# Attention in a hybrid S5 and sliding-window block: four buffers for transposed P, and the transposes ahead of P times V

## What is computed

```python
ATTN_PATTERNS = ((128, 1), (512, 4), (2048, 16))       # window, dilation; 8 heads of 64 each
proj = rmsnorm(x, norm_mix_g) @ w_in                    # u for the S5 branch, q k v, two gates
q = rmsnorm(q, q_norm_g) * scale;  k = rmsnorm(k, k_norm_g)
# per pattern and head, in blocks of 128 queries against the 256 keys that end with them
s = q_blk @ k_blk.T + bias                              # causal window and slope per head
p = exp(s - max(s));  den = sum(p);  o = (p @ v_blk) / den;  lse = max(s) + log(den)
o_attn = sum over patterns of softmax(lse) * o
```

## Time and profile before

| | |
|---|---|
| time, median of 3 runs | 1765.79 us (1765.23 to 1767.33) |
| the profiled execution | 1766.91 us |
| its span, first to last instruction | 1764.8 us |
| PE busy | 1720.0 us, 97% |
| DVE, ACT, POOL busy | 61%, 38%, 51% |
| PE waiting for ACT ptr L1601 | 5.4 us ahead of L1204, 1.6 us ahead of L1215 |
| attention stage | about 50 to 650 us of the span |

### The profile page before, as it was taken

The page is one execution under the profiler, slowest core; times in us unless marked ns, Lnnn a source line. Parts: engine busy times, 40 slices in busy tenths (PEclk is TensorE's granted clock), DMA queues, the critical chain, the costliest instruction groups (busy, mean ns, idle before and its releaser), DMA issues.

```text
span 1764.8 us, 23387 instructions
## 1 busy us (share of the span) xinstructions
PE 1720.0 (97%) x8316; PEld 1376.5 (78%) x8316; DVE 1073.0 (61%) x1553; ACT 664.5 (38%) x1263; POOL 902.9 (51%) x668
## 2 busy tenths in 40 slices
PE   8999999999999987999999999999999999999999
PEld 6777777777777765788887788788888888888887
DVE  6444555564455558443316632688778778748999
ACT  6653455445345521111411121443333333344443
POOL 7545463635544356664276754255545545445554
PEclk9999999999999998999999999999999999999999
DMA  4111321321132034444576534323223222385443
GB/s 180 37 43 34 96 79 43 90 67 55 30 99 73 25 97 109 121 121 121 217 250 245 194 131 166 132 99 104 71 71 93 85 71 73 137 274 165 138 144 126
DMA packets 89690, 198.84 MB, mean 113 GB/s; under 512 B 16560, under 2 KB 34096, under 8 KB 89600
## 3 DMA queue, kind: packets, MB, share of 16 engines
q1 hardware_dynamic: 78496, 190.19, 33.5%
q10 hardware_dynamic: 10640, 5.84, 1.4%
q0 software_dynamic: 464, 1.62, 0.2%
HBM read 152.31 MB, written 44.12 MB: 111 GB/s over the span
## 4 chain that ended last, share of the span: by engine, by line
PE 73%; DVE 14%; DMA 4%; POOL 3%; issue 2%; ACT 2%; SPq 0%; DVEq 0%; POOLq 0%; ACTq 0%
PE bank L1069 13%; PE bank L1071 12%; PE bank L1070 12%; PE bank L1422 7%; PE bank L1424 7%; PE bank L1423 7%; DVE dalo L2321 3%; DMA ab<-wgt_scr 2%; PE bank L1204 2%; PE bank L1215 2%; PE bank L1487 1%; PE bank L1488 1%; PE bank L1486 1%; PE bank L1188 1%; DMA raw<-in_wblocks 1%
## 5 line engine op out<-in xcount | busy, mean ns | idle before, releaser
L1069 PE MATMUL bank<-hhi,whi 128*128 128x512 f32 x1024 | 419.2, 409 | 11.6 <-DVE zb L1975 4.5
L1071 PE MATMUL bank<-hhi,wlo 128*128 128x512 f32 x1024 | 405.9, 396 | 0.0
L1070 PE MATMUL bank<-hlo,whi 128*128 128x512 f32 x1024 | 405.6, 396 | 0.0
L784 POOL TENSOR_TENSOR wlo<-raw,whi 128x1024 fp32r<-128x1024 f32 (+1 forms) x84 | 198.1, 2358 | 380.1 <-DVE whi L1859 378.6
L1069 PEld LDWEIGHTS bank<-hhi,whi 128*128 128x128 f32 x1024 | 194.0, 189 | 59.5 <-issue 6.6
L1071 PEld LDWEIGHTS bank<-hhi,wlo 128*128 128x128 f32 x1024 | 193.7, 189 | 45.9
L1070 PEld LDWEIGHTS bank<-hlo,whi 128*128 128x128 f32 x1024 | 194.5, 190 | 40.0 <-issue 0.2
L1058 POOL TENSOR_TENSOR dwlo<-dw_raw,dwhi 128x512 fp32r<-128x512 f32 x77 | 112.0, 1457 | 104.0 <-ACT dwhi L1751 104.0
L1614 ACT ACTIVATE sp<-sp,sd 128x128 f32<-128x128 f32 (+1 forms) x192 | 84.3, 440 | 117.4 <-DVE sd L2039 117.1
L1486 PE MATMUL bank<-dahi,dwhi 128*128 128x512 f32 x308 | 119.9, 389 | 0.0
L1487 PE MATMUL bank<-dalo,dwhi 128*128 128x512 f32 x308 | 119.8, 389 | 0.0
(11 more groups left out here) (319 smaller groups left out, 3739.3 us busy)
## 6 DMA issues: line engine op xcount, KB each, us to landing
raw<-in_wblocks SPq DMA_DIRECT2D x76, 512.0 KB, 4.4
pair<-in_wblocks SPq DMA_DIRECT2D x40, 512.0 KB, 4.8
ws<-in_wblocks SPq DMA_DIRECT2D x22, 512.0 KB, 5.3
wsum_scr<-ws SPq DMA_DIRECT2D x22, 512.0 KB, 3.9
ff_scr<-ffo SPq DMA_DIRECT2D x22, 512.0 KB, 5.9
dw_raw<-wsum_scr SPq DMA_DIRECT2D x44, 256.0 KB, 2.7
ff<-ff_scr SPq DMA_DIRECT2D x36, 256.0 KB, 4.1
dw_raw<-in_wblocks SPq DMA_DIRECT2D x33, 256.0 KB, 3.2
```

The source lines that it names most:

```text
L784: pool.tensor_tensor(wlo[par][:, 0:cols], raw[par][:, 0:cols], whi[par][:, 0:cols].bitcast(F32), ALU.subtract).then_inc(lo_done, 1)
L1069: nc.tensor.matmul(ps, a, x, start=start and k == k_list[0], stop=False)
L1070: nc.tensor.matmul(ps, a, y, start=False, stop=False)
L1071: last = nc.tensor.matmul(ps, b, x, start=False, stop=stop and k == k_list[-1])
```

## The change

`ptr` gets four buffers in place of two: a second tensor of the same size, `ptr_b`, is allocated beside scratch of the attention stage. ScalarE's copy and P times V choose the buffer by the block number modulo 4. On PE the transposes of block j-2 are moved ahead of P times V of blocks j-4 and j-3 within the sub-step. All waits stay with their instructions.

```diff
@@ tensors
-            ptr = sb("ptr", [P, 2, HT])
+            ptr_a = sb("ptr_a", [P, 2, HT])
...
+                ptr_b = sb("ptr_b", [P, 2, HT])
...
+        ptr = [x[:, i, :] for x in (ptr_a, ptr_b) for i in range(2)]
@@ PE, slot
+                        if 2 <= j < 10:
+                            s_ = j - 2
+                            pe.wait_ge(exp_done, 8 * a + s_ + 1)
+                            if a or s_:
+                                pe.wait_ge(tev, 8 * a + s_)
+                            for x in range(2):
+                                for kb in range(keys(ag, s_) // P, 2):
+                                    c = (2 * x + kb) * P
+                                    last = nc.tensor.transpose(b_t[:, c:c + P], sp[:, s_ % 4, x, kb * P:(kb + 1) * P], ident)
+                            last.then_inc(t_done, 1)
                         if j in (4, 6, 8, 10):
...
-                                                                ptr[:, s_ % 2, c:c + P], start=kb == k0, stop=kb == 1)
+                                                                ptr[s_ % 4][:, c:c + P], start=kb == k0, stop=kb == 1)
                                 last.then_inc(pv_done, 1)
-                        if 2 <= j < 10:
...
-                            last.then_inc(t_done, 1)
@@ ACT, slot
-                        src, dst = (... for x in (b_t[:], ptr[:, s_ % 2, :]))
+                        src, dst = (... for x in (b_t[:], ptr[s_ % 4]))
```

More of the change, by code:

```diff
@@ L1599, in slot @@
                         act.wait_ge(t_done, 8 * a + s_ + 1)
-                        src, dst = (x.rearrange("p (h q) -> p h q", h=2)[:, :, keys(ag, s_):] for x in (b_t[:], ptr[:, s_ % 2, :]))
+                        src, dst = (x.rearrange("p (h q) -> p h q", h=2)[:, :, keys(ag, s_):] for x in (b_t[:], ptr[s_ % 4]))
                         act.activation(dst, src, ACT.Copy).then_inc(tev, 1)
```

## The result

The changed kernel takes 1775.12 us in the median (1774.24 to 1777.44), the kernel before, measured beside it, 1766.56: a ratio of 1.0050 with a 95% interval of 1.0035 to 1.0065. Measured a second time it took 1775.58 us against 1767.38, a ratio of 1.0055 (1.0034 to 1.0076). The ratios here are not exactly those of the medians: the medians alone differ by 8.6 and 8.2 us, the ratios by 0.50% and 0.55% (8.8 and 9.7 us), each with an interval of 2.6 to 3.7 us to either side. The prediction was 1774.6.

What follows compares the result with a forecast made beforehand. PE, busy for 97% of the span, was taken to bound the kernel. The terms 1.9 + 3.5 + 3.5 = 8.9 us, on the scale of the median 1765.79, gave 1774.6 us, range 1768.0 to 1779.5.

Steps and rivals of the forecast that it cites:

- What bounds the kernel: Whole span: PE is busy for 97%, so a microsecond on its queue is normally one of the total.
- the no-change rival: Waits behind the attention stage, for zb and wlo, take up the loss: 1765.8 to 1768 us; chance 0.13.
- (a) The switch: Unstalled j = 4 and 6: entering the split array behind full-array transposes costs 0.17 us, eleven times, 1.9 us.
- The cover for the other five sub-steps: At j = 4 of slots 2, 3, 5, 6, 8 the loss falls into a later wait and costs nothing.
- (b) Stalls that lost their cover: Copy waits inside P times V, slots 2, 3, 5, 6, 8, 9: 0.49 to 0.74 us each, together 3.5.
- (c) The hidden wait: At j = 8 of eight slots, transposes wait for a copy the first PV half covered: 3.5 us.
- The last slot: PE gains 2.3 us at j = 4, 6 and 8, given no value because later waits grow.
- the sum: Slots 0 to 10: switches 1.9, stalls 3.5 and j = 8 waits 3.5 make 8.9 us, 0.5%.
- the two signs that would have shown the theory wrong: Exponentials starting earlier relative to S at j = 4 or 6, or transposes to PV under 0.4 us.
- Early copies: Attention stage: earlier transposes bring later copies forward and the eight stalls go, giving 1762.5 us; chance 0.08.
- The clock: Behind the two long waits, more PE idling prolongs the low clock, at most 3.5 us: 1778; chance 0.12.

Runs made afterwards that it cites:

- the split order: Against the kernel with only the four buffers: transposes put between the two halves of P times V; 1773.81 us against 1766.46, ratio 1.0050.
- the second trace: The changed kernel run and traced once more, with nothing altered; measured a second time at 1775.58 us against 1767.38, ratio 1.0055.
- the first experiment: Kernel before with four buffers for the transposed P, transposes still behind P times V; 1765.92 us against 1765.99, ratio 1.0001.
- early copies: ScalarE's copy ahead of its squares: kernel before 1769.41, again 1767.52 us; changed kernel 1770.26; kernel before, j = 3 and 5 only, 1764.03.

## Why the prediction was right, point by point

**What bounds the kernel.** PE's time was added to the total one for one. From the start of the last slot to the end of the wait for wlo it took 65.3 us before and 64.8 after, 65.3 with the new order in the last slot alone. In all thirteen traces it is 64.7 to 65.3 us, while the wait for zb varies from 2.5 to 5.2. That end follows the slot's start and not PE's arrival, so the no-change rival falls: the 10.3 us of slots 0 to 10 all arrive behind.

**(a) The switch.** Forecast 0.17 us in eleven sub-steps, 1.9 us. Ten of the eleven show 0.15 to 0.20 and sum to 1.6; the eleventh, j = 6 of slot 9, holds a stall. The Trainium skill ("TensorEngine Tiling (Array Packing)", Tiling Modes, Key Properties) has a change of tiling mode drain the engine; the 0.58 us in place of 0.41 agrees with it, and so do the two extra switches of the split order. The cover for the other five sub-steps held in four: slots 3 and 6 took the loss at j = 4 back at j = 6, slot 8 at j = 5, and slot 5 had none (-0.30 and 0.17 at j = 4 and 5). The fifth, slot 2, is below.

**(b) Stalls that lost their cover.** Forecast 0.49 each for slots 2, 5 and 8: measured 0.47, 0.46, 0.45. Forecast 0.74 for slots 3 and 6: measured 0.81 and 0.63, by both stalled sub-steps together, of which 0.5 stands at j = 4 and the rest at j = 6. Slot 9 at j = 4: forecast 0.53, measured 0.50. In sum 3.3 for 3.5.

**(c) The hidden wait.** Forecast 0.4 in each of eight slots and 0.1 more in three: measured 0.41 and 0.42 in five, 0.45 to 0.48 in three, 3.5 us as forecast. Alone it costs 3.3 us of time. The wait is shown; that its size came out so well is partly luck, because two errors cancelled. The forecast took 0.10 off for the switch from projection to P times V that is gone. But PE waits for the copy in that place, so nothing is saved there. What is saved lies behind: the one transpose of the maxima and sums at j = 8 is a column-split matmul too (128*32), which the prediction did not see. Before, in slot 0:

```profile
93.81 0.66 PE L1215 MATMUL bank<-cst_s,sp 128*128 128x128 f32 x4
94.31 0.27 PE L1220 MATMUL bank<-cst_s,sd 128*32 128x128 f32 x1
94.34 0.48 PE L1069 MATMUL bank<-hhi,whi 128*128 128x512 f32 x1
```

The transposes of P take 0.50 us to it where they take 0.41 to a projection, so entering that mode costs 0.09. Changed, P times V stands ahead of it and takes 1.08, as ever: this entry is gone. By these rows slot 0 loses 0.14 us by the switch to P times V (0.55 for 0.41) and gets 0.09 back, so some 0.35 of its 0.41 is the late restart.

**The last slot.** The place was right and the size off: PE passed it 1.3 us sooner, not 2.3. I had not seen that at j = 8 the transposes would meet ACT's copy of block 5 in the open there too; that wait is 1.0 us. It did no harm: of the 1.3 us 0.7 stand in the longer wait for zb, and the 0.5 by which the end of the wait for wlo comes sooner lie within the 64.7 to 65.3 us over which it varies from trace to trace.

**What the sum did not hold.** Its terms sum to 8.4 us in the trace, the trace shows 10.5. Slot 9 at j = 6 gave 1.3 and slot 2 at j = 4 and 5 gave 1.1, of a broadcast of ab that landed about a microsecond later; in the second trace slot 2 has half of that. Small gains elsewhere take 0.3 off. These are places that move from trace to trace. In time the two measurements gave 8.6 and 8.2, the sum 8.9. That the forecast of 1774.6 hit the median to 0.5 us is in part luck, then: the interval reaches 2.6 us to either side, and the forecast stands on one trace, whose stalls at j = 6 do not all repeat.

**The signs.** Of the two signs that would have shown the theory wrong, one did not come: transposes to P times V take 0.55 to 0.59 at full keys, not under 0.4. The other came by its letter in two places: at j = 6 of slots 3 and 6 ScalarE's exponentials start 0.4 to 0.6 us earlier after S than before (and at j = 4 of slots 5 and 8, 0.15 and 0.07). But counted from the slot's start those of slots 3 and 6 stand where they stood, to 0.1 us; it is S that starts 0.5 later.

**The rivals.** Early copies: the waits did not go, and the buffers alone changed nothing. The copy of the same sub-step does end earlier, in slot 0 by 0.3 us at j = 4 and by 0.5 at j = 6 from the slot's start, but the next one, for which PE waits, does not. As for buffers, the rule of the Trainium skill on repeating gaps ("Perfetto Trace Analysis", Optimization Strategy) did not hold for the buffers of `ptr`, as the first experiment shows. The waits ahead of the transposes are another matter: there PE waits until the one bank `b_t` has been copied out. A second bank for the transposes was not tried, so what it would give stays open. What did shorten PE's waits for the copy was the order on ScalarE. The clock: behind the two long waits, where that rival had its place, it was granted 0.78 as before, and the span's mean was 0.993 after 0.994. The same 27 us of the changed kernel, 10 us later:

```profile
673.00:700.00 27.00, 20.68 (x91) 16.75 (x92) 22.12 (x20) 3.76 (x9) 19.44 (x10) 0.78 0.61 143
```

## What to carry to other kernels

Work that stands ahead of a wait covers it: before moving an instruction that waits ahead of one that doesn't, read for each occurrence when the awaited thing is ready, including those that show no wait today. Count the changes between full, row-split and column-split matmuls in the new order, and price them from a place where the trace shows one. More buffers of a kind help only if some wait in the trace is for a free one of that kind. Here no wait was for a free `ptr`; P times V waited for a copy held behind other work on its engine, and moving two of these copies gave 0.2%.

## What the runs showed of the hardware

A small VectorE instruction can take more than ten times as long beside a GpSimd one, by a hair. At j = 4 of slot 9 VectorE negates four maxima (sd, 128 x 4). In the kernel before (order of time) it started 0.08 us ahead of GpSimd's tensor_tensor on 128 x 512 and took 0.18 us:

```profile
542.42 0.18 DVE L2039 TENSOR_SCALAR sd<-mx 128x4 f32<-128x4 f32 x1
542.50 2.20 POOL L929 TENSOR_TENSOR num<-num,ab 128x512 f32<-128x512 f32 x1
```

In the changed kernel it started 0.02 us behind, and took 2.08, to just behind the end of the other:

```profile
550.00 2.07 POOL L931 TENSOR_TENSOR num<-num,ab 128x512 f32<-128x512 f32 x1
550.02 2.08 DVE L2041 TENSOR_SCALAR sd<-mx 128x4 f32<-128x4 f32 x1
```

The same pair stands in slots 3, 6 and 9 of all thirteen traces, 39 places. In 28 the VectorE instruction took 2.08 to 2.19 us and ended 0.02 to 0.04 behind GpSimd's; it had started between 0.01 ahead of it and 0.04 behind. In 11 it took 0.17 to 0.20 us; it had started between 0.12 ahead and level.

The exponentials, the squares and the copy of the slot wait for it. With the copy in its old place the stall at j = 6 stands in every slot where it was long and in none where it was short. With early copies the loss, at j = 6 or 8, stands where it was long, but for 0.3 us in one slot.

When it starts is set by a DMA. Some 6 us earlier VectorE waits in each of these slots for `ab` to land, and the instruction starts 6.0 to 6.1 us after that. VectorE goes on, with the copy in its old place, 15.14 to 15.21 us after the slot's start where the instruction was short and 15.22 to 15.45 where it was long. So a tenth of a microsecond in a DMA's landing can become 1.2 us of PE's time, and single traces of these kernels differ by that much without any change. No run moved this pair alone: the link rests on the 39 places and on the chain of waits between them and PE.
